# Both feed-forward products of a hybrid decoder layer as seven block products

## What is computed

```
D_FF = 4 * D_MODEL            # 4096, D_MODEL = 1024, SEQ = 512
h = h + jnp.concatenate([y_a, y_b], axis=-1) @ w_out[i]      # mixer
hid = jax.nn.relu(rmsnorm(h, norm_mlp_g[i]) @ w_ff1[i])      # first product
h = h + (hid * hid) @ w_ff2[i]                               # second product
gate = jax.nn.sigmoid(rmsnorm(h, ple_norm_g[i]) @ w_ple_gate[i])
h = h + gate * (p[i] @ w_ple_proj[i])
return rmsnorm(h, final_norm_g)
```

## Time and profile before

| | |
|---|---|
| median of three runs | 748.49 us (748.48 to 748.50) |
| profiled execution | 747.09 us |
| its span | 745.3 us |
| mean granted clock of PE, share of full speed | 0.997 |
| PE busy in the span | 735.0 us, 99% |
| DVE busy | 454.1 us |
| ACT busy | 382.9 us |
| feed-forward units | 364.4 to 691.5 us, 327.1 us |

### The profile page before, as it was taken

The page is one execution under the profiler, slowest core; times in us unless marked ns, Lnnn a source line. Parts: engine busy times, 40 slices in busy tenths (PEclk is TensorE's granted clock), DMA queues, the critical chain, the costliest instruction groups (busy, mean ns, idle before and its releaser), DMA issues.

```text
span 745.3 us, 8676 instructions
## 1 busy us (share of the span) xinstructions
PE 735.0 (99%) x3396; PEld 606.4 (81%) x3396; DVE 454.1 (61%) x500; ACT 382.9 (51%) x516; POOL 107.3 (14%) x88
## 2 busy tenths in 40 slices
PE   8999999999999999999999999999999999999996
PEld 7888877788878888888888888888888888888884
DVE  5556794576667465546444952576454942589764
ACT  6524456644674833304564633572266524575775
POOL 1031000766455000000012000020001000200000
PEclk9999999999999999999999999999999999999998
DMA  9732223342241163100976685477727792585311
GB/s 332 210 86 86 87 85 99 124 143 86 93 162 57 57 214 125 58 29 14 373 234 148 140 297 150 84 143 231 227 63 156 192 275 97 118 192 178 106 57 56
DMA packets 47872, 105.58 MB, mean 142 GB/s; under 512 B 4668, under 2 KB 6360, under 8 KB 47832
## 3 DMA queue, kind: packets, MB, share of 16 engines
q1 hardware_dynamic: 40968, 84.03, 33.7%
q0 software_dynamic: 5632, 16.78, 12.4%
q10 hardware_dynamic: 1232, 4.23, 1.6%
HBM read 88.21 MB, written 4.23 MB: 124 GB/s over the span
## 4 chain that ended last, share of the span: by engine, by line
PE 98%; DMA 1%; ACT 0%; issue 0%; DVE 0%; SPq 0%; DVEq 0%
PE acc L1487 28%; PE acc L1489 28%; PE acc L1488 28%; PE side L1549 3%; PE side L1488 2%; PE side L1489 2%; PE side L1487 2%; PE side L1646 2%; PE side L1613 1%; PE side L1653 1%; PE side L1641 1%; DMA gain<-in_norm_mix_g 1%; PE acc L1570 0%; PE side L1593 0%; PE side L1594 0%; PE side L1633 0%
## 5 line engine op out<-in xcount | busy, mean ns | idle before, releaser
L1487 PE MATMUL acc<-w_hi,a_hi 128*128 128x512 f32 x256 | 104.5, 408 | 0.0
L1489 PE MATMUL acc<-w_hi,a_lo 128*128 128x512 f32 x256 | 100.2, 391 | 0.0
L1488 PE MATMUL acc<-w_lo,a_hi 128*128 128x512 f32 x256 | 99.9, 390 | 0.0
L1487 PE MATMUL acc<-b_hi,ring_hi 128*128 128x512 f32 x256 | 99.7, 390 | 0.0
L1489 PE MATMUL acc<-b_hi,ring_lo 128*128 128x512 f32 x256 | 99.7, 389 | 0.0
L1488 PE MATMUL acc<-b_lo,ring_hi 128*128 128x512 f32 x256 | 99.7, 389 | 0.0
L664 ACT ACTIVATE ring_hi<-quarter 128x1024 fp32r<-128x1024 f32 x56 | 56.5, 1051 | 51.3 <-PE acc L1489 34.7
L1293 DVE TENSOR_TENSOR ring_lo<-ring_raw,ring_hi 128x1024 fp32r<-128x1024 f32 x32 | 38.6, 1223 | 67.0 <-ACT ring_hi L664 67.0
L1293 DVE TENSOR_TENSOR ring_lo<-quarter,ring_hi 128x1024 fp32r<-128x1024 f32 x56 | 66.0, 1220 | 17.0 <-ACT ring_hi L664 17.0
L568 POOL DMA_DIRECT2D quarter<-quarter x24 | 20.8, 868 | 351.1 <-DMA quarter<-in_w_ff 223.1
L993 DVE TENSOR_TENSOR w_lo<-w_raw,w_hi 128x1024 fp32r<-128x1024 f32 (+1 forms) x40 | 50.8, 1272 | 27.9 <-ACT w_hi L587 27.4
(11 more groups left out here) (231 smaller groups left out, 1471.8 us busy)
## 6 DMA issues: line engine op xcount, KB each, us to landing
quarter<-in_w_ff SPq DMA_DIRECT2D x40, 512.0 KB, 4.8
w_raw<-in_w_in SPq DMA_DIRECT2D x36, 512.0 KB, 3.7
ring_raw<-in_w_ff SPq DMA_DIRECT2D x32, 512.0 KB, 4.9
quarter<-quarter POOLq DMA_DIRECT2D x24, 512.0 KB, 6.1
w_raw<-in_w_out SPq DMA_DIRECT2D x16, 512.0 KB, 3.4
h<-in_x SPq DMA_DIRECT2D x8, 512.0 KB, 4.3
seg<-cs_dram ACTq DMA_DIRECT2D x8, 512.0 KB, 3.9
quarter<-in_w_ff POOLq DMA_DIRECT2D x8, 512.0 KB, 6.3
```

Source lines behind the costliest of these rows:

```text
L1487: pe.matmul(dst, st[0], mv[0], start=start, stop=False)
L1488: pe.matmul(dst, st[0], mv[1], start=False, stop=False)
L1489: return pe.matmul(dst, st[1], mv[0], start=False, stop=stop)
```

## The change

The second product keeps its scheme with another order, and the first product gets the same scheme with the roles exchanged: the normalized x is the factor that is the same in all units, so its blocks and sums (`x_hi`, `x_lo`) are made once. A form of the first product is now a 512x512 block or sum of w_ff1, multiplied by a 512x256 block of x: 48 matmuls of 128x256 per block product, seven a unit, 336 matmuls instead of 192. Banks are used in pairs (`pair`), two results of 256 columns in a bank. The seven results are put together into four blocks of hidden values by seven DVE operations (`combine`) and two ACT copies out of PSUM (`copy_product`, P1 and P3); relu and square follow as one ACT operation of 128x1024 each per block (`hidden`).

A unit has 14 forms instead of 11. `ring_raw` is gone: the four quarters serve both products. T3, T2 and T4 are adding transfers between quarters in both products, twelve a unit; T1 is made on DVE (`make_t1`, quarter 1 minus quarter 3, two pieces per product, four a unit). There are 16 loads a unit. Before unit 0 come `x_evac`, `x_sum` and `x_split`. In the last unit, T4 is second to last, and `h_finish` x6 and `h_add` of T4 stand behind each other on DVE before the last product's banks are read.

```diff
-STEPS = 30
-FORMS = 11
-PRODUCTS = ("B11", "T3", "T2", "T1", "T4", "B21", "B22")
-A_FORMS = ("A11", "S3", "S2", "S1", "A22", "A12", "S4")
+FORMS = 14
+FIRST = ("B11", "B21", "B22", "T2", "T3", "T1", "T4")
+FIRST_A = ("A11", "A12", "S4", "S2", "S3", "S1", "A22")
+SECOND = ("B11", "B21", "T3", "T2", "T1", "T4", "B22")
+SECOND_A = ("A11", "A12", "S3", "S2", "S1", "A22", "S4")
 QUARTER = {"T3": 0, "T1": 0, "B12": 0, "B11": 1, "T2": 1, "T4": 1, "B21": 2, "B22": 3}
-SUMS = ("T3", "T2", "T1", "T4")
...
+            def load_quarter(u, m, name):
...
-                if u:
-                    last = {0: "T1", 1: "T4", 2: "B21", 3: "B22"}[i]
-                    sp.wait_ge(form_lo, form_count(u - 1, last, 1))
+                if u or m:
+                    v, q = (u, 0) if m else (u - 1, 1)
+                    user = {0: "T1", 1: "T4", 2: "B21", 3: "B22"}[i]
+                    sp.wait_ge(form_lo, form_count(v, q, user, 1))
+                    if name == "B21":
+                        for p in range(2):
...
+                        sp.wait_ge(t1_made, 4 * u + 2)
                 elif i < 2:
                     sp.wait_ge(lo_ready, 4 * (PLE + 1))
...
+            for u in range(UNITS):
+                load_quarter(u, 1, "B22")
+                load_quarter(u, 1, "B12")
+                load_quarter(u, 1, "B21")
+                load_quarter(u, 1, "B11")
+                if u < UNITS - 1:
+                    load_quarter(u + 1, 0, "B21")
+                    load_quarter(u + 1, 0, "B12")
+                    load_quarter(u + 1, 0, "B11")
+                    load_quarter(u + 1, 0, "B22")
...
-            def t_add(u, name, p):
...
-                k = 8 * u + 2 * p
                 if name == "T3":
-                    pool.wait_ge(q_landed[0][p], 16 * (2 * u + 1))
...
                 elif name == "T2":
-                    sum_landed(pool, u, "T3", p)
-                    pool.wait_ge(form_lo, form_count(u, "B11", p))
+                    sum_landed(pool, u, m, "T3", p)
+                    pool.wait_ge(form_lo, form_count(u, m, "B11", p))
                     src = quarter[0][at]
-                elif name == "T1":
-                    pool.wait_ge(q_landed[0][p], 16 * (2 * u + 2))
-                    src = w_ff2[:, k:k + 2, 0:512]
...
-                    pool.wait_ge(q_landed[2][p], 16 * (u + 1))
+                else:
+                    pool.wait_ge(form_lo, form_count(u, m, "T2", p))
+                    pool.wait_ge(q_landed[2][p], quarter_count(u, m, "B21"))
+                    pool.wait_ge(t1_made, 4 * u + 2 * m + p + 1)
                     src = quarter[2][at]
                 pool.dma_start(quarter[QUARTER[name]][at], src, accum_op=ALU.add
                                ).then_inc(t_landed[QUARTER[name]][p], 16)
...
+                for m in range(2):
+                    for name in ("T3", "T2", "T4"):
+                        for p in range(2):
+                            t_add(u, m, name, p)
...
+                act.activation(t, t, ACT.Square).then_inc(hid_raw, 1)
             def split_a(u, name):
...
-                    act.wait_ge(hid_raw, 8 * u + 4)
-                    act.activation(a11_hi[:], a1[:, :, 0:256], ACT.Copy).then_inc(hid_hi, 1)
-                elif name[0] == "A":
-                    k = 0 if name == "A2a" else 2
-                    act.wait_ge(hid_raw, 8 * u + 8)
-                    act.activation(a2[0][:, k:k + 2, :], a2[1][:, k:k + 2, :], ACT.Copy).then_inc(hid_hi, 1)
-                else:
...
+                def both(j):
                     for p in range(2):
-                        split_form(n + 1, p)
-                for i in range(4):
...
+                both(2)
+                if u == 0:
+                    x_split("S3")
+                    x_split("S1")
+                copy_product(u, "P1")
+                both(3)
+                if u == 0:
+                    x_split("A22")
+                both(4)
+                hidden(u, "A11")
+                copy_product(u, "P3")
                 split_a(u, "A11")
-                for p in range(2):
-                    split_form(n + 4, p)
+                both(5)
+                both(6)
+                both(7)
...
+                hidden(u, "A12")
+                split_a(u, "A12")
+                both(9)
+                hidden(u, "A21")
+                hidden(u, "A22")
                 split_a(u, "S3")
-                for p in range(2):
-                    split_form(n + 5, p)
-                for i in range(4, 8):
-                    relu(u, i)
...
-                    split_form(n + 6, p)
+                both(10)
                 split_a(u, "S2")
                 split_a(u, "S1")
...
-                split_a(u, "A2b")
...
                 split_a(u, "S4")
-                for p in range(2):
...
+                both(11)
+                both(12)
+                both(13)
                 if u < UNITS - 1:
-                    for p in range(2):
-                        split_form(n + FORMS, p)
+                    both(14)
+                    both(15)
...
+            def make_t1(u, m, p):
+                at = (slice(None), slice(2 * p, 2 * p + 2))
+                sum_landed(dve, u, m, "T2", p)
+                dve.wait_ge(form_lo, form_count(u, m, "T3", p))
+                dve.tensor_tensor(quarter[0][at], quarter[1][at], quarter[3][at], ALU.subtract).then_inc(t1_made, 1)
...
+            def combine(u, what):
+                dst, left, right, op = {
+                    "C11": ("A11", "A21", pair(1), ALU.add), "U": ("A21", pair(1), "A21", ALU.subtract),
+                    "C12 part": ("A12", "A12", "A21", ALU.add), "U3": ("A21", "A21", pair(0), ALU.add),
...
+                    "C21": ("A21", pair(0), "A21", ALU.subtract)}[what]
+                left, right = [f_raw[t][:] if isinstance(t, str) else t for t in (left, right)]
+                if what == "C11":
+                    dve.wait_ge(p_copied, 2 * u + 1)
+                elif what == "C12 part":
+                    dve.wait_ge(p_copied, 2 * u + 2)
+                if COMBINED.index(what):
+                    dve.wait_ge(combined, combined_count(u, what) - 1)
+                if what != "C12 part":
+                    name = {"C11": "B21", "U": "T2", "U3": "T3", "C12": "T1", "C22": "T1", "C21": "T4"}[what]
+                    dve.wait_ge(ff_step, product_end(u, 0, name))
+                dve.tensor_tensor(f_raw[dst][:], left, right, op).then_inc(combined, 1)
...
-                    for p in range(2):
-                        split_form(n + 1, p)
+                both(2)
+                if u == 0:
+                    x_split("S3")
+                    x_split("S1")
+                both(3)
+                if u == 0:
+                    x_split("A22")
+                combine(u, "C11")
+                both(4)
                 for p in range(2):
-                    split_form(n + 2, p)
+                    make_t1(u, 0, p)
+                both(5)
+                split_a(u, "A11")
+                combine(u, "U")
+                combine(u, "C12 part")
+                both(6)
+                combine(u, "U3")
...
+                both(7)
+                combine(u, "C12")
+                combine(u, "C22")
+                both(8)
+                combine(u, "C21")
+                split_a(u, "A12")
+                both(9)
+                s_add(u, "S3")
+                s_add(u, "S1")
+                split_a(u, "S3")
+                s_add(u, "S2")
+                s_add(u, "S4")
+                both(10)
...
                 split_a(u, "S2")
+                h_add(u, "B21")
                 split_a(u, "S1")
-                split_a(u, "A2a")
-                split_a(u, "A2b")
...
+                both(11)
                 h_add(u, "T3 right")
                 h_add(u, "T3 above")
+                both(12)
+                split_a(u, "A22")
+                h_add(u, "T2")
+                both(13)
...
-                    split_form(n + 10, p)
+                if last:
+                    for what in LAST_ADDS:
+                        h_finish(what)
+                else:
+                    both(14)
                 h_add(u, "T4")
-                if u < UNITS - 1:
...
+                if not last:
...
+                n = FORMS * u + j
+                hi, lo = ring[n % 3]
+                name = FIRST_A[j]
...
+                elif u == 0:
+                    pe.wait_ge(xf_lo, X_ORDER.index(name) + 1)
+                if j < 2:
+                    pe.wait_ge(*((h_added, add_count(u - 1, ("T4", "B22")[j])) if u else emptied(PLE, 2 + j)))
+                elif j in (2, 4):
+                    pe.wait_ge(p_copied, 2 * u + j // 2)
+                else:
+                    pe.wait_ge(combined, combined_count(u, {3: "C11", 5: "U", 6: "U3"}[j]))
...
                     for k in range(4):
                         if i == 0 and k % 2 == 0:
                             pe.wait_ge(form_lo, 2 * n + k // 2 + 1)
```

(15 more changed lines are left out.)

587 lines of the change are left out of this document (294 added, 293 removed).

## The result

The changed kernel takes **795.45 us** (median of four runs, 791.24 to 797.75) against 748.49 before: a ratio of 1.063, 95% interval 1.058 to 1.067. The forecast was 768.0 with a range of 746 to 789. The direction is right, the time lies above the range. The profiled execution took 795.12 us with a span of 793.4, 48.1 more than before.

What follows compares the result with a forecast made beforehand. PE was taken to bound the kernel, busy 99% of the span. Four units of -4.5 + 8.0 give +14.0; with +3.0 and +2.5 at the ends, +19.5 on 747.1; plus 1.4 to the median, 768.0 us, range 746 to 789.

Steps and rivals of the forecast that it cites:

- PE's own work: PE in each feed-forward unit: 77.1 us, 4.5 less than before, with a 128x256 matmul at 0.116 us.
- the upper bound: 128x256 matmul on PE: 0.120 us if each matmul pays the fixed 0.0133; a unit then saves 3.2 us.
- DVE's run: 15 DVE operations from C21 to h_add of B21: 18.3 us against PE's 16.3; PE waits at least 2.0 to 2.3.
- Transfers: T4's adding transfers through the second product's B11 load and split: 16.2 to 23.0 us, against 19.6 available.
- The stall per unit: PE's waits in the second product, at B11, B21, T3 and T2: 3.4 to 10.2 us, taken as 8.0.
- backlog: DVE held by B11's late split, so C21 starts 1.1 to 7.9 us late.
- The clock: PE's clock falls in waits over some 2.3 us, costing 2.4 each, 8 times: +19, 787; chance 0.12.
- the main case: The forecast's own case: units of 77.1 us with 5 to 10 of stall, 752 to 782; chance 0.65.
- the rival: Clock falling in PE's waits, 8 x 2.4 = +19 us, 787 in all; chance 0.12.
- The ends: Unit 0's third block product waits for P1's copy, +3.0 us; last unit's last product waits for DVE, +2.5.
- Transfers covered: Rival: T4 and B11 transfers land like lone ones, only 2.3 us of stall remain per unit: 739.6; chance 0.19.
- Weight loads showing under the narrow matmul: Rival: 128x256 matmuls on PE too short to cover weight loads, 0.188 us each: 840.8; chance 0.04.

Runs made afterwards that it cites:

- the best kernel: Changed kernel with loads ordered B21, B11, B22, B12, h_add of B21 ahead of make_t1, and ACT and DVE queues sorted: 764.75 us, 1.0240 of the kernel before.
- the first two orders of loads: The changed kernel's own order, and B11 ahead of B12 and B21; with h_add moved ahead of make_t1: 799.42 and 788.14 us, without 795.45 and 785.49.
- the third: Changed kernel with second product's loads ordered B21, B11, B22, B12: 783.08 us; with h_add moved ahead of make_t1 as well, 779.70 us.

## Why the forecast was too low

**PE's own work.** The step that took 0.116 for a 128x256 matmul was mis-sized: 0.120, 1.3 us per unit, 5.4 in all. The argument for the upper bound (a fixed part paid by every matmul) was the right one; the middle between it and the rate of small matmuls was not evidence.

**DVE's run.** Right in place. From C21 to `h_add` of B21 DVE ran without a pause, 15 operations as counted, and T2 waited 3.7 us against "about 4". (The working gives 18.3 - 16.3 = 2.0 for this run; the 2.3 that the prediction goes on with has no row.) In the trace of the changed kernel (timeline of DVE, unit 1):

```profile
478.51 2.36 DVE L1412 TENSOR_TENSOR quarter<-quarter 128x1024 f32<-128x1024 f32 x2
...
494.27 1.22 DVE L1431 TENSOR_TENSOR fS_raw<-fS_raw,acc 128x1024 f32<-128x1024 f32 x1
505.89 2.36 DVE L1405 TENSOR_TENSOR ring_lo<-quarter,ring_hi 128x1024 fp32r<-128x1024 f32 x2 [10.41 <-ACT ring_hi L748]
508.17 1.22 DVE L1431 TENSOR_TENSOR fA_raw<-fA_raw,acc 128x1024 f32<-128x1024 f32 x1
509.42 1.22 DVE L1431 TENSOR_TENSOR fA_raw<-fS_raw,acc 128x1024 f32<-128x1024 f32 x1
...
512.83 1.22 DVE L1431 TENSOR_TENSOR fS_raw<-acc,fS_raw 128x1024 f32<-128x1024 f32 x1
...
525.63 2.35 DVE L1412 TENSOR_TENSOR quarter<-quarter 128x1024 f32<-128x1024 f32 x2
...
529.03 1.22 DVE L1469 TENSOR_TENSOR h<-h,acc 128x1024 f32<-128x1024 f32 x1
```

From C21's start at 512.83 to the end of `h_add` at 530.25 are 17.4 us; the prediction had 18.3. The first product had ended at 503.6, so C21 came 9.2 late where 1.1 to 7.9 was forecast.

**Transfers.** Right in place, too short in size. DVE idled 10.4 us ahead of B11's split, with C12 and C22 right behind it. T4's second adding transfer took 10.6 us, where the earlier trace rows gave 9.0 as the longest, and B11's loads 10.4 and 11.1 (tile quarter, 494.3 to 495), where the earlier trace rows gave 8.8:

```profile
L513 SPq DMA_DIRECT2D quarter<-in_w_ff x2: 368/543/718, 494.4 to 494.8; - x2
...
DMA to landing us min/median/max: 10.4/10.8/11.1
```

From the first piece of `make_t1` (done at 479.7) to the end of B11's split it was 28.6 us against 16.2 to 23.0. `make_t1` itself came 0.9 us before the fourth block product began, not 2.7 behind it, or the backlog would have been longer still: 28.6 + 4.5 for four operations on DVE - 23.9 to the end of the first product = 9.2. The rows came from stretches with fewer transfers at a time; here two adding transfers and up to four loads were under way. The order of the loads alone brought the 10.6 back to 6.1, which shows the crowding to be its cause.

**The stall per unit** is a term that was mis-sized, though its waits look right: 8.4, 7.7 and 8.6 us in units 1 to 3 against 8.0, in the pieces 3.6 to 3.8 (B11), 0 to 0.9 (B21), 0.3 (T3) and 3.7 (T2). From the end of the first product to the start of T2 each unit lost more than these waits, 11.0, 10.4, 10.6 and 10.5 us over the 16.3 of PE's work, in unit 1 the 9.2 of backlog and DVE's run of 17.4. That is above the prediction's upper bound of 10.2. From B11's split on (505.9) DVE runs through to `h_add`, which T2 waits for, so T2 starts when DVE is done, as long as PE gets there first. The slow matmuls behind B11's wait (1.7 to 2.9) took the place of waiting: unit 2 has 2.7 of them and 7.7 of waits, units 1 and 3 have 1.7 and 8.4 and 8.6. That the waits came to the forecast 8 is luck.

**The clock** is the step that failed together with it. The prediction had waits of "about 4 us" in the main case, took some 2.3 as the point from which the clock decides (PE's last work ends at 738.15 and the clock is down by 740.4), and then left the clock out of the sum, as a rival with a chance of 0.12: by its own rows the main case and the rival were one. The slow matmuls came to 19.0 us, and the rival had 8 x 2.4 = 19. This agreement is luck too: they stood behind ten waits ahead of block products, not eight, at 1.4 to 2.9 each, and 9.8 of them lay between a unit's first product and T2, where they took the place of waits. The kernel with `h_add` moved shows the same in unit 0, up to which both are alike: its third product had 1.3 less of slow matmuls behind it, the next wait (for U3, behind T4's split, whose adding transfer took 12.4) was 3.3 instead of 2.2, and the product behind that began only 0.3 earlier.

**The whole miss.** The profiled time grew by 48.0 where 19.5 was forecast, 28.5 more. PE's own work is 5.4 of it, the four stalls 10.6 (42.6 against 32.0), the slow matmuls behind the four T2 6.5 (against nothing), unit 0's first product 4.8 (7.8 against 3.0, with the second wait of 2.2 and 2.9 of slow matmuls), and what is left, 1.2, lies at the end and behind the feed-forward part. So the largest steps are two: transfers beside each other taken as too short, and the clock put at nothing.

**The ends.** Unit 0's third block product waited 2.7 against 3.0; the end waited 2.3 against 2.5.

**The rivals.** Transfers covered: no. With T4's adding transfers and B11's loads out of the crowd T3's were late instead, and T2 still waited in the best kernel. Weight loads showing under the narrow matmul: no, 0.120.

## What to carry to other kernels

Less work on PE brought nothing here, since the engines that feed it work in a ring with it: the scheme saved 12.8 us of PE and lost more than four times that in waits and slow matmuls. Where a wait of 2 us or more in one piece is forecast on PE, price it twice, once for itself and once for the clock behind it, unless another wait follows whose end something else sets: that one takes the slow matmuls in. Several waits under 1.5 us (0.1 to 0.2 lost behind each) are cheaper than one of 4 (2.4 to 2.6 behind it in the kernel before). Take a transfer's time from a stretch that is as crowded as the new one will be. And a queue that is served in order should hold first what is there first: sorting the queues of ACT and DVE behind a better order of loads gave 31 of the 47 us back. A new order of the loads alone gave 10 and 12 us of it. Moving `h_add` ahead of `make_t1`, which takes one wait away and delays the start of a ring, cost 3 to 4 with the first two orders of loads and gained 3 with the third.
